# The second pass of an mLSTM layer, from channels on partitions to tokens on partitions

## What is computed

```python
s = jnp.einsum('bhtd,bhsd->bhts', qc, kc) * jnp.exp(dmat - m_t[..., None])
w_inter = jnp.exp(inter - m_t)
num = jnp.einsum('bhts,bhse->bhte', s, vc) + w_inter[..., None] * jnp.einsum('bhtd,bhde->bhte', qc, C)
den = jnp.sum(s, axis=-1) + w_inter * jnp.einsum('bhtd,bhd->bht', qc, n)
h = num / jnp.maximum(jnp.abs(den), jnp.exp(-m_t))[..., None]
...
C_new = decay[..., None, None] * C + jnp.einsum('bhsd,bhse->bhde', kw, vc)
n_new = decay[..., None] * n + jnp.sum(kw, axis=2)
```

## Time and profile before

| | us |
|---|---|
| median of 3 runs (lowest, highest) | 2508.53 (2508.32, 2511.76) |
| the profiled execution, its own time | 2508.7 |
| its span in the profile | 2506.9 |
| TensorE busy in the span | 2247.3 (90%) |
| VectorE, ScalarE, GpSimd busy | 1130.5, 821.4, 548.7 |
| mean granted clock of TensorE | 0.927 of full |
| second pass: first broadcast at 1208.41, first output panel at 1917.88 | 709.5 |
| output panels, to 2033.5 | 115.6 |

### The profile page before, as it was taken

One profiled execution on the slowest core, in us unless ns is written; L12 is line 12 of the kernel. 1 busy time (PEld: TensorE's weight loads), 2 busy tenths in 40 slices (PEclk: granted clock), 3 DMA queues, 4 the chain that ended last, 5 costly groups with the idle time before them and its releaser, 6 DMA issues.

```text
span 2506.9 us, 35392 instructions
## 1 busy us (share of the span) xinstructions
PE 2247.3 (90%) x14144; PEld 1822.5 (73%) x14144; DVE 1130.5 (45%) x2078; ACT 821.4 (33%) x1722; POOL 548.7 (22%) x440
## 2 busy tenths in 40 slices
PE   6899998979999979798799999999997979999886
PEld 3788876969898868686457557567566968888675
DVE  2577764134555541755333143232325134777532
ACT  3355553043444431312302303203112033565412
POOL 0323201324224223232101102002013532222120
PEclk9899997989999989899799989989898988999888
DMA  7212213213223133234022123032124221102001
GB/s 283 59 45 75 70 45 101 61 47 100 62 76 89 55 104 45 73 114 150 19 62 91 66 82 129 25 105 84 42 75 164 76 62 44 29 19 62 18 26 42
DMA packets 294203, 186.52 MB, mean 74 GB/s; under 512 B 50174, under 2 KB 267559, under 8 KB 294063
## 3 DMA queue, kind: packets, MB, share of 16 engines
q1 hardware_dynamic: 277374, 156.18, 21.3%
...
## 4 chain that ended last, share of the span: by engine, by line
PE 79%; DVE 7%; ACT 7%; DMA 3%; issue 2%; SPq 1%; ACTq 0%; DVEq 0%
PE pc L1348 18%; PE acc L1290 18%; PE acc L628 4%; PE acc L1440 4%; PE acc L1429 4%; PE acc L612 3%; PE acc L550 3%; PE pt L1451 3%; PE acc L586 2%; PE acc L1297 2%; PE acc L1635 2%; PE pc L1312 2%; PE acc L1647 2%; DMA raw<-in_w_mod 1%; PE pc L617 1%
## 5 line engine op out<-in xcount | busy, mean ns | idle before, releaser
L1213 POOL TENSOR_TENSOR idle<-eps 128x1 f32<-128x1 f32 x144 | 42.8, 297 | 1870.8 <-PE acc L1290 779.8
L1348 PE MATMUL pc<-hh,wh 128*128 128x320 f32 x1152 | 380.4, 330 | 38.2 <-DVE hl L2228 35.2
L1216 POOL TENSOR_TENSOR wl<-raw,wh 128x1024 fp32r<-128x1024 f32 x144 | 361.1, 2508 | 11.5
L1348 PE MATMUL pc<-hh,wl 128*128 128x320 f32 x1152 | 363.3, 315 | 0.0
L1348 PE MATMUL pc<-hl,wh 128*128 128x320 f32 x1152 | 363.3, 315 | 0.0
L1348 PEld LDWEIGHTS pc<-hh,wh 128*128 128x128 f32 x1152 | 223.7, 194 | 50.9 <-issue 26.4
L1348 PEld LDWEIGHTS pc<-hl,wh 128*128 128x128 f32 x1152 | 223.9, 194 | 0.2 <-issue 0.2
L1348 PEld LDWEIGHTS pc<-hh,wl 128*128 128x128 f32 x1152 | 222.9, 194 | 0.0
L1290 PE MATMUL acc<-hh,wh 128*128 128x320 f32 x640 | 152.6, 320 | 32.4 <-DVE hl L1053 17.0
L1214 POOL CAST wh<-raw 128x1024 fp32r<-128x1024 f32 x144 | 154.0, 1070 | 0.0
L1290 PE MATMUL acc<-hl,wh 128*128 128x320 f32 x640 | 148.4, 314 | 0.0
...
## 6 DMA issues: line engine op xcount, KB each, us to landing
raw<-in_w_mod SPq DMA_DIRECT2D x144, 256.0 KB, 3.5
raw<-in_gqa_w_in SPq DMA_DIRECT2D x80, 256.0 KB, 3.5
raw<-in_diff_w_in SPq DMA_DIRECT2D x64, 256.0 KB, 4.0
raw<-in_mlstm_w_in SPq DMA_DIRECT2D x64, 256.0 KB, 3.5
...
raw<-in_gqa_w_out SPq DMA_DIRECT2D x32, 256.0 KB, 3.3
raw<-in_state_mlstm_C SPq DMA_DIRECT2D x32, 256.0 KB, 3.6
...
```

Of the source, the lines that this page charges most:

```text
L1216: pool.tensor_tensor(wl[:, s], raw[:, r], wh[:, s].bitcast(F32), ALU.subtract).then_inc(w_full[s], 1)
L1348: ins = pe.matmul(pc[:, c:c + 320], w[:, sl, kt, :], h[:, kt, t:t + 320], start=kt == 0 and n == 0, stop=kt == KT - 1 and n == 2)
```

## The change

Tokens are put on partitions from the numerators on. A step (`STEPS`: direction and query tile of 128 tokens) now makes 128 tokens by 512 channels: queries are the stationary operand with C0 as the moving one, and triangle tiles are stationary with the values as moving. Both `mv` and the C0 slots (`CS`, five of them in place of two) have a 513th column, ones and n0, so the denominator falls out of the same matmuls, which are 256 and 257 columns wide. VectorE has weights as columns (`tiny`, from `ccol`), adds both directions into `hs`, and takes mean and variance with its moments instructions. ScalarE scales the part from the initial state in forward steps and normalises; TensorE turns the result back by 20 transposes a head. The broadcasts of `bmrow` and `wirow`, the matmuls with ones, the centring and the sum of squares go. The modulation panels take the form that the other layers use, one behind each of the first six steps. Gate panels are done in halves into `pc`. Head 3 comes first, with xm and xc left in SBUF from the first pass, and its queries, keys and values are made inside the serial piece. Four buffers of a head's size (`rot`, `blocks`) change their roles from head to head. In the last head the gates come ahead of the steps, and the first output panels come among its last stages. The loops over heads are written out. The per-head copies of columns (`hcol`) go.

```diff
+        ORDER = (MH - 1, *range(MH - 1))
+        STEPS = ((0, 1), (0, 2), (0, 3), (0, 4), (None, 0), (1, 4), (1, 3), (1, 2), (1, 1))
...
+                for m in (2, 3, 4):
+                    mod_item(p, m)
+                for kt in (1, 2, 3):
+                    initial(p, 1, kt)
+                mod_item(p, 5)
+                if p < MH - 1:
+                    gate_panel(p, 2)
+                    gate_panel(p, 3)
+                    sp.wait_ge(h_done, NST * (p + 1))
+                    sp.dma_start(blocks(p + 2)[:, :, 0:T], scratch["xc"][ORDER[p + 1]].rearrange("b p t -> p b t")).then_inc(xc_full, 16)
+                    first_initials(p + 1)
+                    sp.wait_ge(ym_ready, MB * (p + 1))
+                    sp.dma_start(scratch["y"][ORDER[p] * MB:ORDER[p] * MB + MB].rearrange("b p t -> p b t"), blocks(p + 1)[:, :, 0:T])\
+                        .then_inc(y_spill, 16)
+                    sp.wait_ge(y_spill, 16 * (p + 1))
+                    sp.dma_start(blocks(p + 1), scratch["xm"][ORDER[p + 1]].rearrange("b p t -> p b t")).then_inc(xm_full, 16)
...
+            def step(p, s):
+                b = take(p, "n", s, h_done, NST * p + s + 1)
+                lo, hi, far = acc[b][:, 0:512], acc[b][:, 512:1024], pt[:, 512 * b:512 * b + 512]
+                def mm(dst, lhsT, rhs, start, stop):
+                    return pe.matmul(dst, lhsT, rhs, start=start, stop=stop, skip_group_check=True)
+                d, tau = STEPS[s]
+                if d is None:
+                    for e in range(2):
+                        a = amat[:, e * AW:e * AW + P]
+                        mm(lo[:, 256 * e:256 * e + 256], a, mv[:, 0, 0:256], True, True)
+                        ins = mm((hi, far)[e][:, 0:257], a, mv[:, 0, 256:513], True, True)
+                else:
+                    mq = blocks(p + 2)
                     for kt in range(4):
...
+                        n = 8 * p + 4 * d + kt
+                        pe.wait_ge(c_full[n % 5], 32 * (n // 5 + 1))
+                        q = mq[:, kt, tau * P:(tau + 1) * P]
+                        mm(lo[:, 256:512], q, CS[n % 5][:, 0:256], kt == 0, kt == 3)
+                        ins = mm(far[:, 0:257], q, CS[n % 5][:, 256:513], kt == 0, kt == 3)
+                        if s in (3, NST - 1):
+                            ins.then_inc(c_used[n % 5], 1)
+                    order = range(1, tau + 1) if d == 0 else range(tau, QT)
+                    for j, i in enumerate(order):
+                        c0, _, o = tri(d, i)
+                        a = amat[:, d * AW + o + tau * P - c0:d * AW + o + tau * P - c0 + P]
+                        mm(lo[:, 0:256], a, mv[:, i, 0:256], j == 0, j == len(order) - 1)
+                        ins = mm(hi[:, 0:257], a, mv[:, i, 256:513], j == 0, j == len(order) - 1)
                 ins.then_inc(acc_full[b], 1)
...
+            def mod_sum(p, m):
+                slot, j = m % 2, m // 2
+                at = 512 * (j % 2) + P * (m % 2)
+                if m == 4:
+                    pe.wait_ge(*seen.at(mod_read, 3 * p + 1))
+                pe.wait_ge(*seen(raw_full[slot], 32))
+                for kt in range(KT):
+                    g = 32 * (kt % 4)
+                    ins = pe.matmul(pc[g:g + 32, at:at + P], cond32[:, kt, :], raw[:, slot, kt, :], start=kt < 4, stop=kt >= 4,
+                                    skip_group_check=True)
+                ins.then_inc(mod_summed, 1)
...
+            def state(p, d):
+                if d == 0:
+                    pe.wait_ge(kw_ready, 2 * p + 2)
+                for kb in range(MB):
+                    b = take(p, "s", MB * d + kb, cst_copied, 8 * p + MB * d + kb + 1)
+                    pe.matmul(acc[b][:, 0:256], ht[:, d, kb * P:(kb + 1) * P], mv[:, 0, 0:256], start=True, stop=True)
+                    pe.matmul(acc[b][:, 512:769], ht[:, d, kb * P:(kb + 1) * P], mv[:, 0, 256:513], start=True, stop=True)\
+                        .then_inc(acc_full[b], 1)
+            def turned(p, *blks):
+                hs = rot(p + 3)[:, 0:QT * MD].rearrange("p (t e) -> p t e", e=MD)
+                pe.wait_ge(hn_ready, QT * (p + 1))
+                for blk in blks:
+                    b = take(p, "T", blk, t_read, MB * p + blk + 1)
+                    for t in range(QT):
+                        ins = pe.transpose(acc[b][:, t * P:(t + 1) * P], hs[:, t, blk * P:(blk + 1) * P], ident)
+                    ins.then_inc(acc_full[b], 1)
+            def out_panel(r, i):
...
+            queries_keys(0, 0, 2)
+            pe.wait_ge(g_copied, 1)
+            for n in range(2):
+                pair(lambda o, w: (pc, pt)[n][0:64, o:o + w], place[:, n * 64:n * 64 + 64], lambda c0, c1: g16[:, c0:c1], True, True)\
+                    .then_inc(place_full, 1)
+            queries_keys(0, 2, 2 * MB)
+            values(0)
+            pe.wait_ge(rows_ready, 1)
+            pe.wait_ge(row_read, 1)
...
+            for p in range(MH):
+                broadcasts(p)
+                if p:
+                    queries_keys(p, 0, 2 * MB)
+                products(p)
+                if p:
+                    values(p)
+                panels_taken(0, 1)
...
+                            gate_unit(p, blk, half)
+                    panels_taken(0, 1)
+                    seen.back(pe, ("c", 0))
+                    seen.back(pe, ("c", 1))
+                for s in range(NST):
+                    step(p, s)
+                    if s < 6:
+                        mod_sum(p, s)
+                    if s in (3, 5, 7):
+                        mods_turned(p, (s - 3) // 2)
+                if p < MH - 1:
+                    panels_taken(0, 1)
+                    seen.marks[("c", 0)] = seen.at(mod_read, 3 * p + 3)
+                    seen.marks[("c", 1)] = seen.at(mod_read, 3 * p + 2)
+                    gate_unit(p, 0, 0)
+                    gate_unit(p, 0, 1)
+                    state(p, 0)
+                    gate_unit(p, 1, 0)
+                    gate_unit(p, 1, 1)
+                    state(p, 1)
+                    gate_unit(p, 2, 0)
+                    gate_unit(p, 2, 1)
+                    gate_unit(p, 3, 0)
+                    turned(p, 0, 1)
+                    gate_unit(p, 3, 1)
+                    turned(p, 2, 3)
+                else:
+                    out_panel(0, 0)
...
+                b = RING[(p, "n", s)] % 2
+                act.activation(rinv[:, 0:256], acc[b][:, 256:512], ACT.Copy, scale=tiny[:, s % 2, 3:4])
...
+                for t in range(QT):
+                    act.activation(hs[:, t, :], hs[:, t, :], ACT.Identity, bias=rstd[:, 1, t:t + 1], scale=rstd[:, 0, t:t + 1]).then_inc(hn_ready, 1)
...
+            def weight_of(p, s, d, tau, den, qn):
+                col, t = (lambda k: ccol[:, p % 2, d, k + tau:k + tau + 1]), tiny[:, s % 2, :]
+                if qn is not None:
+                    step(dve.tensor_scalar(t[:, 0:1], qn, col(WIC), None, ALU.mult))
+                    step(dve.tensor_tensor(t[:, 0:1], den, t[:, 0:1], ALU.add))
+                    den = t[:, 0:1]
+                step(dve.tensor_scalar(t[:, 1:2], den, -1.0, col(EMC), ALU.mult, ALU.max))
+                step(dve.tensor_tensor(t[:, 1:2], den, t[:, 1:2], ALU.max))
+                step(dve.reciprocal(t[:, 2:3], t[:, 1:2]))
+                if qn is not None:
+                    dve.tensor_tensor(t[:, 3:4], t[:, 2:3], col(WIC), ALU.mult).then_inc(rw_ready, 1)
+                    dve.wait_ge(rw_ready, 8 * p + (s + 1 if s < 4 else s))
+                return t[:, 2:3], t[:, 3:4]
+            def moments(p, t):
+                hs = rot(p + 3)[:, 0:QT * MD].rearrange("p (t e) -> p t e", e=MD)
+                step(dve.bn_stats(bnp[:, t % 2, :], hs[:, t, :]))
...
+                else:
+                    r, rw = weight_of(p, s, d, tau, hi[:, 256:257], far[:, 256:257])
                     if d == 0:
...
+                        dve.wait_ge(t1_ready, 4 * p + s + 1)
+                        scaled(ha, lo[:, 0:256], r, rinv[:, 0:256])
+                        ins = scaled(hb, hi[:, 0:256], r, rinv[:, 256:512])
+                    else:
+                        dve.wait_ge(h_done, NST * p + s)
+                        scaled(ha, lo[:, 256:512], rw, ha)
+                        step(scaled(hb, far[:, 0:256], rw, hb))
+                        scaled(ha, lo[:, 0:256], r, ha)
+                        ins = scaled(hb, hi[:, 0:256], r, hb)
+                ins.then_inc(h_done, 1)
+                if d != 0:
+                    dve.wait_ge(h_done, NST * p + s + 1)
+                    ins = moments(p, tau)
+                    if s == NST - 1:
+                        ins.then_inc(var_ready, 1)
```

1020 lines of the change are left out of this document (523 added, 497 removed).

## The result

The kernel after takes 2334.16 us (median of 4 runs, 2329.07 to 2336.43) against 2508.45 us (2508.32 to 2511.76): a ratio of 0.9299, with a 95% interval from 0.9282 to 0.9317. It is 174 us faster; the forecast was 218.8 us less than before, 2290 us, with 2328 as the upper end. The sign and the main mechanism were right, and 44 us of the expected gain are missing. Its profiled execution has a span of 2334.6 us, its last output matmul ends at 1861.6 us, where 1816.0 was forecast, and the last layer behind it takes 473.0 us (473.4 before). So the missing part lies whole ahead of that matmul.

What follows compares the result with a forecast made beforehand. TensorE, busy 773 of 852 us, bounds the second pass: its work, gaps and low clock. Lead-in, heads (125.3 us in the middle) and end put the last output matmul at 1816.0; 2508.7 - 218.8 = 2290 us, range 2268 to 2328.

Steps and rivals of the forecast that it cites:

- y of head 2 is fetched under 40 us of panels: Output panels: today's 17.00 us gap goes with the store and load it waits for.
- rival B: Second pass: transfers come late, each state waiting again for 4-byte n0 DMAs, 32 us in all, 2322 us; chance 0.12.
- TensorE's work: Second pass, heads: matmul columns at 1.69 ns sum to 120.0 us a head, against 174 to 175 now.
- Modulation: Six panels a head in other layers' form, 5.4 us with small matmuls, for 18.4 before plus low clock behind.
- VectorE's step: Steps: 3.1 us forward, 3.7 backward, against TensorE's 4.3 to 6.9; only the context step waits, 0.5 us a head.
- Rival A: Steps: VectorE becomes the bound, a backward step takes 6 us, TensorE waits 16 us in all, 2306 us; chance 0.14.
- Waits that are left: Heads 1 to 3: key copies 3 us, last values 0.8, state copy 1, context step 0.5; 5.3 us a head.
- The end: From head 3's last step to the last output matmul: 125.5 us, including 3 us of waits for ScalarE and VectorE.
- Lead-in: Before the first step: steps start at 1234.5 instead of 1250.8 us; query matmuls in the serial chain add 2 us.
- C: Steps: the two banks do not overlap, TensorE waits for VectorE each step, 133 us, 2423 us; 0.05 with halfway cases.
- D: Steps: granted clock falls, slower than before if 46% of TensorE's work runs low, 2578 us at 60%; chance 0.03.
- The 1.3 us of the first pass: First pass, head 0: twenty small copies ahead of the matrices TensorE waits for go, 1.3 us less.

Runs made afterwards that it cites:

- e8: Kernel after with eight output panels ahead of y's wait, keys before weights, n as rows, earlier m stores, later normalising in heads 0 to 2: 2288.42 us, ratio 0.9116.
- e10: The kernel after run once more with no edit, on the same chip as e9 and e11: 2338.72 us, ratio 0.9334.
- e4: Kernel after with modulation panels in the old form (weight tile stationary, two columns moving), still placed between the steps: 2346.69 us, ratio 0.9353.
- e9: e4 plus the old place of the modulation panels (two clusters of three) and their weight loads behind the initial state's: 2395.16 us, ratio 0.9554.
- e7: Kernel after with each 512-column moments instruction issued four times, 2.1 us more VectorE per context and backward step: 2348.68 us, ratio 0.9351.
- e6: Kernel after with four useless 256-column matmuls in TensorE's wait ahead of the products in heads 1 to 3: 2326.70 us, ratio 0.9260.
- e2: Kernel after without the 32 stores of new n: 2311.78 us, ratio 0.9215.
- e11: Kernel after with new n turned by one transpose a direction and stored as 4 rows of 512 bytes, 8 stores for 32: 2313.01 us, ratio 0.9235.
- e5: Kernel after with the first head's queries, keys and values made behind the broadcasts, not in the lead-in's serial piece: 2340.99 us, ratio 0.9324.

## Why the prediction was right or wrong

Three steps of the prediction failed. It priced each wait of TensorE by its length alone, with nothing for the low clock behind it. It took the loads at the end as hidden ("y of head 2 is fetched under 40 us of panels"), where SyncE's queue stood still behind the last stores. And it had the 32 stores of new n at nothing in its sum and only as rival B. From the first step to the last output matmul its sum was 581.5 us, of which 18.6 were waits and 562.9 TensorE's work. The kernel after takes 625.7: 39.1 us idle, 20.5 more than counted, and 586.6 busy, 23.7 more. Of these 23.7 us the low clock has 14.2, as e8 gets them back by shorter waits; 9.5 stay in e8 at a clock of 1.00 and are work that the sum priced too low.

- **TensorE's work: right to 2%.** Steps with modulation were forecast at 52.2 us a head and 0.5 of waits; 53.1 measured. Gates 28.4 for 28.2. Output panels 7.05 each. A head in the middle has 122.2 us of work in e8 (two small transposes of n among them) for 120.0. That e8 has its last output matmul at 1816.9 where the sum said 1816.0, and takes 2288 us for 2290, is in part luck: it has 9.5 us more work than the sum and 8.8 us fewer waits (9.8 for 18.6), and its last layer took 468.8 us where the sum has the 473.4 of the kernel before.
- **Modulation: the total right, the reason wrong.** 18.4 us came down to about 5.4, as in the sum. With 4.4 us for the clock behind, the text expected 17.4 us a head or 70 in all; undoing it cost 64 (14 and 50), or 55 against e10. But the text gave most of this to the form; e4 and e9 give 4.35 us a head to the form and some 12 to the place, which ended a wait for the third panel's weights with its low clock. The rows showed it: in the earlier trace rows the first two panels take 3.63 us and the third, behind a wait of 2.06, alone 3.57.
- **VectorE's step: right.** 3.1 us forward as forecast, 4.0 backward for 3.7; the bounds of the moments held, at their lower end. Rival A did not occur: of its prices (0.35 us for a small operation, 1.4 for the moments, 0.48 for a product) the trace has 0.16 to 0.22, 0.69 and 0.44 to 0.48. e7 adds its 2.1 us behind the point where the banks come free; that this holds up no step in three heads shows slack there, and what slower products would cost was not tried.
- **Waits that are left: the key copies right, the clock behind them left out.** 3 us for the key copies measured 3.30, the state copy 1.78 to 2.03 instead of 1. The failed step is that each wait was priced by its length alone. Behind the keys' waits the products lose another 1.5 to 2.7 us to the clock in each of three heads, as e6 shows by filling the idle time. The lead-in's products were put at 15.5 us and took 17.24.
- **Rival B: it occurred, at 0.12, and its price came from a far row.** It had each state wait once more for the 4-byte DMAs to land, 32 us in all. Its 4.04 us of the earlier trace rows are two stores of m, 4 pieces each; a store of n, 128 pieces, lands after 4.9 to 13.0 us (median 8.7). State copies waited four times for that, 14.3 us, most of which TensorE did not see; no initial state was late. What the rival did not have is the queue of the engine that issues them: a pair takes 1.3 to 3.7 us of ScalarE, which delays copies and gates (TensorE's 3.15 us ahead of the third output panel stand behind one issue of 2.56), and the store of y beside them lands after 15.4 us instead of 6.8. Without the stores, or with rows in their place, the kernel is 16 to 30 us faster by the times, whichever run of the kernel after is taken (e2, e11). The kernel before has 8 stores of n, each a row of 2 KB, and its C stores land in 3.2 us; that the change makes 32 stores of columns of them stood in the diff.
- **The end: wrong, the largest miss.** The sentence on y of head 2 followed the load and not SyncE's queue. The sixth weight panel stands behind the wait for y and m on that queue. 9.49 us of wait and 4.5 us of slow panels behind it (112.8 for 98.8) are 14 of the 19.7 us. Ahead of the third panel TensorE waits 5.9 us in all, 3.15 of them for state copies, where 3 were counted.
- **Lead-in: the sum right, two of its terms not.** From L577 to the first step it was to take 58.3 us (from 1176.21 in the profile before) and takes 57.7. The two query matmuls ahead of the placing were priced at 2 us; in fact queries, keys and values with their copies cost the serial piece 6.4 (e5). Without them it would have been shorter than before, 26.2 us for 31.2: VectorE's scans of `bmrow` take 3.07 us in e5 where they took 5.85, and the first scan of `mrow` 0.41 where it took 2.44, 4.8 of the 5.0 us.
- **The other rivals.** C did not occur: TensorE's only wait of note in a head's steps is one of 0.37 us behind the context step. D did not occur: the steps run at 1.00 in every head, though the two pairs of banks change hands at each of the nine. The Trainium skill (TensorE: Matmul & The Clock Gate, A second HAM failure mode: psum-queue depth-cycling) warns of such cycling with small idles; the steps have hardly any (52.7 of 53.1 us busy), so this trace is no test of the warning. In this layer's second pass the clock fell only behind waits. The 1.3 us of the first pass cannot be read, since its end moves by more than that.
- **The range.** It reached to 2328, as A and B were taken one at a time and the clock behind waits had no term. With the 14 us that e8 shows for it, forecast and upper end would have been 2304 and 2342.
